# The forgetting attention turns two key tiles in one run and then makes both value products

## The reference, cut to what matters

```python
F = jnp.cumsum(logf, axis=-1)
def block(args):
    qi, Fi, i = args
    logits = (jnp.einsum('bhqd,bhkd->bhqk', qi, k) * scale + Fi[..., :, None] - F[..., None, :])
    logits = jnp.where(kpos[None, :] <= qpos[:, None], logits, -jnp.inf)
    p = jax.nn.softmax(logits, axis=-1)
    return jnp.einsum('bhqk,bhkd->bhqd', p, v)
...
y_f = h_f.reshape(B, S, F_W) * jax.nn.silu(f_z)
y = jnp.concatenate([y_m, y_f], axis=-1) @ w_out[l]
```

## Time and profile before

| | |
|---|---|
| Time, median of 3 runs | 1593.19 us (1592.62 to 1593.48) |
| Span of the profiled execution (no other time is on record for it) | 1588.2 us |
| TensorE, matmul | 1515.7 us busy, 95% |
| TensorE, weight load | 1152.1 us, 73% |
| VectorE | 792.8 us, 50% |
| ScalarE | 533.7 us, 34% |
| POOL | 174.9 us, 11% |
| Mean granted TensorE clock | 0.985 |
| Share of the chain that ended last: scores, turns, products of the attention | 7%, 7%, 8% |

### The profile page before, as it was taken

How to read it: one execution, slowest core, us unless ns; L and a number is a source line. 1 busy time by engine, 2 the same in 40 slices (tenths; PEclk the granted TensorE clock), 3 DMA queues, 4 the chain that set the end, 5 groups by cost and what they waited for, 6 DMA issues and landing times.

```text
span 1588.2 us, 21410 instructions
## 1 busy us (share of the span) xinstructions
PE 1515.7 (95%) x7913; PEld 1152.1 (73%) x7913; DVE 792.8 (50%) x1835; ACT 533.7 (34%) x812; POOL 174.9 (11%) x237
## 2 busy tenths in 40 slices
PE   2999999999899999999999899999999997999998
PEld 2677877887788888888888665555555555888886
DVE  5845445321120100355541585766766747677674
ACT  4842323201111111222211566565655644222220
POOL 2000000002000000000000312103112000222121
PEclk8999999999999999999999999999999998999999
DMA  9313133241341311121232534223161037576761
GB/s 346 133 32 131 68 132 112 101 145 34 107 149 61 99 67 65 42 79 53 79 132 80 151 102 133 54 75 126 45 177 46 16 91 241 175 189 184 182 198 54
DMA packets 128569, 178.09 MB, mean 112 GB/s; under 512 B 8764, under 2 KB 90824, under 8 KB 123416
## 3 DMA queue, kind: packets, MB, share of 16 engines
q1 hardware_dynamic: 119488, 129.75, 27.5%
q0 software_dynamic: 9008, 47.36, 7.9%
HBM read 116.93 MB, written 60.16 MB: 112 GB/s over the span
## 4 chain that ended last, share of the span: by engine, by line
PE 80%; DVE 8%; ACT 5%; DMA 3%; issue 2%; POOL 1%; SPq 0%; DVEq 0%; POOLq 0%; ACTq 0%
PE a_ps_u L703 26%; PE a_ps_u L745 14%; PE m_ps_out L1804 11%; PE f_ps_o L1341 8%; PE f_ps_t L1316 7%; PE f_ps_s L1304 7%; PE a_ps_u L727 1%; DVE stage L481 1%; DVE u_copy L547 1%; DVE stage L555 1%; ACT work L928 1%; PE m_ps_m L1779 1%; ACT work L930 1%; PE m_ps_m L1780 1%; PE m_ps_m L1783 1%
## 5 line engine op out<-in xcount | busy, mean ns | idle before, releaser
L703 PE MATMUL a_ps_u<-a_h_hi,w_in_hi 128*128 128x512 f32 x736 | 286.9, 390 | 0.9 <-DVEq L519 0.9
L703 PE MATMUL a_ps_u<-a_h_lo,w_in_hi 128*128 128x512 f32 x736 | 286.6, 389 | 0.0
L703 PE MATMUL a_ps_u<-a_h_hi,w_in_lo 128*128 128x512 f32 x736 | 198.1, 389 | 0.0
L703 PEld LDWEIGHTS a_ps_u<-a_h_hi,w_in_hi 128*128 128x128 f32 x736 | 138.1, 188 | 31.8 <-issue 3.2
L703 PEld LDWEIGHTS a_ps_u<-a_h_hi,w_in_lo 128*128 128x128 f32 x736 | 138.2, 188 | 28.8
L703 PEld LDWEIGHTS a_ps_u<-a_h_lo,w_in_hi 128*128 128x128 f32 x736 | 138.2, 188 | 28.2
L745 PE MATMUL a_ps_u<-v_hi,a_h_hi 128*128 128x512 f32 x384 | 150.5, 392 | 6.4 <-ACT stage L957 6.4
L745 PE MATMUL a_ps_u<-v_hi,a_h_lo 128*128 128x512 f32 x384 | 150.3, 392 | 0.0
L437 DVE CAST w_in_hi<-w_in_land 128x1024 fp32r<-128x1024 f32 x24 | 16.6, 691 | 178.4 <-PE a_ps_u L703 93.5
L1474 ACT ACTIVATE f_probs_t<-f_ps_t 128x512 f32<-128x512 f32 (+1 forms) x128 | 65.2, 548 | 98.4 <-PE f_ps_t L1316 98.4
L957 ACT ACTIVATE stage<-a_ps_u 128x512 f32<-128x512 f32 x48 | 28.3, 597 | 198.8 <-PE a_ps_u L745 196.8
(11 more groups left out here) (291 smaller groups left out, 2695.8 us busy)
## 6 DMA issues: line engine op xcount, KB each, us to landing
scratch_arrays<-stage POOLq DMA_DIRECT2D x27, 1024.0 KB, 4.6
scratch_qkT<-stage POOLq DMA_DIRECT2D x8, 2048.0 KB, 7.7
w_in_land<-in_w_in SPq DMA_DIRECT2D x24, 512.0 KB, 7.2
w_in_land<-scratch_arrays SPq DMA_DIRECT2D x32, 256.0 KB, 4.8
m_x_in<-in_x SPq DMA_DIRECT2D x16, 512.0 KB, 4.6
out<-m_result SPq DMA_DIRECT2D x15, 512.0 KB, 3.0
a_ada_rows<-in_w_ada SPq DMA_DIRECT2D x3, 2048.0 KB, 16.5
w_in_land<-in_w_in SPq DMA_DIRECT2D x24, 256.0 KB, 3.3
```

What stands on the lines that cost most here:

```text
L703: ins = pe.matmul(ps_u[:, par, b, :], w[:, k, :], h[:, k, cols], start=(k == 0 and i < 2 * len(blocks) and h is h_hi), stop=(k == KT - 1 a ...
```

## The change

TensorE goes through the steps in groups of two, 2g and 2g+1. In a group it turns steps 2g+2 and 2g+3 in one run and then makes products 2g and 2g+1. If both steps have scores, those of step 2g come before the turns and those of step 2g+1 between the two products; if step 2g has none, or a block ends with the group, all scores of the group come first. So that two steps can be turned ahead, there is a third buffer `probs_t_2`, and `BUFFER[s]` is s modulo 3 below step 150 and s modulo 2 from there on (where, for TensorE, only one step is turned before the first product). A copy of step s waits for the last product that read its buffer (`LAST_READ`). The room for the third buffer comes from `gate_z`, which has two slots of 512 columns instead of four; the z of a block is loaded two blocks ahead, after the block that had its slot was stored. VectorE and ScalarE follow in groups of two steps as well: on VectorE `output`, the first share's logits and `invert` still come first, then the copies of both steps with `gate` behind those of key tile 2, then the second share's logits. The waits for `finished` move from product 0 to the copies of step 1.

```diff
+def z_slot(pair, J):
+    return (pair * TB + J) % 2
...
-    return fox["first_z"] if (pair, J) == (0, 0) else fox["gate_z"][:, J * NB:(J + 1) * NB]
+    slot = z_slot(pair, J)
+    return fox["first_z"] if (pair, J) == (0, 0) else fox["gate_z"][:, slot * NB:(slot + 1) * NB]
...
+        ALL_BUFFERS_UNTIL = EARLY_FROM + 3
+        BUFFER = [s % (len(probs_t) if s < ALL_BUFFERS_UNTIL else 2) for s in range(len(STEPS))]
+        LAST_READ = [max((i + 1 for i in range(s) if BUFFER[i] == BUFFER[s]), default=0) for s in range(len(STEPS))]
...
+        def block_ends(g):
+            return 2 * g + 2 < len(STEPS) and STEPS[2 * g + 2][2] == 0
+
+        def shares(g):
+            first, second = share(2 * g), share(2 * g + 1)
+            return ([*first, *second], []) if block_ends(g) or not first else (first, second)
+
+        def turned_in(g):
+            return [s for s in (2 * g + 2, 2 * g + 3) if s < len(STEPS)]
...
+            def load_next_z(n, J):
+                after_next = group_index(n, J) + 2
+                if 2 < after_next < PAIRS * GROUPS:
+                    load_fox_z(sp, scratch, fox, *divmod(after_next, GROUPS))
...
# TensorE
-            turn(*STEPS[0])
-            for s, step in enumerate(STEPS):
-                more = s + 1 < len(STEPS)
-                if s == EARLY_FROM:
-                    pe.wait_ge(s_used, HP * len(CHUNKS_OF))
-                memory_early(s)
-                new = share(s)
-                for m in new:
-                    scores(m)
-                if more:
-                    turn(*STEPS[s + 1])
-                product(s, *step)
+            for s in range(2):
+                turn(*STEPS[s])
+            for g in range(len(STEPS) // 2):
+                memory_early(2 * g)
+                before, between = shares(g)
+                for m in before:
+                    scores(m)
+                in_turn = turned_in(g)
+                together = len(in_turn) if 2 * g + 2 < ALL_BUFFERS_UNTIL else 1
+                for s in in_turn[:together]:
+                    turn(*STEPS[s])
+                product(2 * g, *STEPS[2 * g])
+                for s in in_turn[together:]:
+                    turn(*STEPS[s])
+                for m in between:
+                    scores(m)
+                product(2 * g + 1, *STEPS[2 * g + 1])
+                if 2 * g + 1 == EARLY_FROM:
+                    pe.wait_ge(s_used, HP * len(CHUNKS_OF))
+                memory_early(2 * g + 1)
...
# VectorE
-            copies(0)
-            for s, (n, J, kt) in enumerate(STEPS):
-                if kt == 0 and s:
-                    output(*STEPS[s - 1][:2])
-                for m in share(s):
-                    logits(m)
-                if kt == 0:
-                    invert(n, J)
-                if s + 1 < len(STEPS):
-                    copies(s + 1)
-                if kt == INV_AT - 1:
-                    gate(n, J)
-                memory_early(s)
+            for s in range(2):
+                copies(s)
+            for g in range(len(STEPS) // 2):
+                n, J, kt = STEPS[2 * g]
+                if kt == 0 and g:
+                    output(*STEPS[2 * g - 1][:2])
+                before, between = shares(g)
+                for m in before:
+                    logits(m)
+                if kt == 0:
+                    invert(n, J)
+                for s in turned_in(g):
+                    copies(s)
+                    if STEPS[s][2] == INV_AT:
+                        gate(*STEPS[s][:2])
+                for m in between:
+                    logits(m)
+                for s in (2 * g, 2 * g + 1):
+                    memory_early(s)
...
# ScalarE
+            for g in range(len(STEPS) // 2):
+                if block_ends(g):
+                    for row in EXPS[2 * g] + EXPS[2 * g + 1]:
+                        exponential(*row)
+                for i, s in enumerate(turned_in(g)):
+                    copies(s)
+                    if not block_ends(g):
+                        for row in EXPS[2 * g + i]:
+                            exponential(*row)
+                for s in (2 * g, 2 * g + 1):
+                    memory_early(s)
```

More of the change, by code:

```diff
@@ L1063, in forgetting_heads @@
         stage_1 = keep["stage"][:, 1]
-        probs_t = [sb("probs_t", [P, HP, NB])[:, :, :], heads(keep["work"][:, HP * NB:2 * HP * NB])]
+        probs_t = [sb("probs_t", [P, HP, NB])[:, :, :], heads(keep["work"][:, HP * NB:2 * HP * NB]), fox["probs_t_2"][:, :, :]]
         inv_wide = stage_1[:, 3 * NB:4 * NB].rearrange("p (r h d) -> p r h d", r=QT, h=HP)
@@ L1212, in _ @@
             load_fox_v(sp, scratch, fox, 1, 0)
-            for J in range(2, GROUPS):
-                load_fox_z(sp, scratch, fox, 0, J)
+            load_fox_z(sp, scratch, fox, 0, 2)
             def store_y(n, J):
@@ L1341, in product @@
                     ins = pe.matmul(ps_o[h * F_DH:(h + 1) * F_DH, first:], v_tok[:, kt, h, :],
-                                    probs_t[s % 2][:, h, first:], start=(kt == 0), stop=(kt == key_tiles(J) - 1))
+                                    probs_t[BUFFER[s]][:, h, first:], start=(kt == 0), stop=(kt == key_tiles(J) - 1))
                 ins.then_inc(pv_done, 1)
@@ L1399, in copies @@
                         dve.wait_ge(t_psum, u + 1)
-                        if s >= 2:
-                            dve.wait_ge(pv_done, s - 1)
-                        dve.tensor_copy(probs_t[s % 2][:, h, first:], ps_t[:, u % T_BANKS, first:]
+                        if s == 1:
+                            dve.wait_ge(after["finished"], U_TILES + 4)
+                        if LAST_READ[s]:
+                            dve.wait_ge(pv_done, LAST_READ[s])
+                        dve.tensor_copy(probs_t[BUFFER[s]][:, h, first:], ps_t[:, u % T_BANKS, first:]
                                         ).then_inc(taken_by_dve, 1)
@@ L1471, in copies @@
                         act.wait_ge(t_psum, u + 1)
-                        if s >= 2:
-                            act.wait_ge(pv_done, s - 1)
-                        act.activation(probs_t[s % 2][:, h, first:], ps_t[:, u % T_BANKS, first:], ACT.Copy
+                        if s == 1:
+                            act.wait_ge(after["finished"], U_TILES + 4)
+                        if LAST_READ[s]:
+                            act.wait_ge(pv_done, LAST_READ[s])
+                        act.activation(probs_t[BUFFER[s]][:, h, first:], ps_t[:, u % T_BANKS, first:], ACT.Copy
                                        ).then_inc(copied_by_act, 1)
@@ L1485, in _ @@
             act.preload_act_table_set("natural_log_exp_and_others")
-            copies(0)
-            for s in range(len(STEPS)):
-                due = s + 1 < len(STEPS) and STEPS[s + 1][2] == 0
-                if due:
-                    for row in EXPS[s]:
-                        exponential(*row)
-                if s + 1 < len(STEPS):
-                    copies(s + 1)
-                if not due:
-                    for row in EXPS[s]:
-                        exponential(*row)
-                memory_early(s)
+            for s in range(2):
+                copies(s)
+            for g in range(len(STEPS) // 2):
+                if block_ends(g):
+                    for row in EXPS[2 * g] + EXPS[2 * g + 1]:
+                        exponential(*row)
+                for i, s in enumerate(turned_in(g)):
+                    copies(s)
+                    if not block_ends(g):
[3 more added lines that the diff above has]
+                    memory_early(s)
             act.wait_ge(y_ready, PAIRS * GROUPS)
```

19 lines of the change are left out of this document (7 added, 12 removed).

## The result

The changed kernel takes 1633.82 us (median of five runs, 1630.40 to 1635.96) against 1593.48 for the kernel before (five runs): a ratio of 1.0245 [1.0231, 1.0259], slower by 40 us. The prediction said 1607.5 us, 1592 to 1621: the sign was right, the size was not, and the measured time lies 13 us above the range. The profiled execution has a span of 1628.7 us, 40.5 over the span of before, so the two traces can be compared directly.

A forecast was written before the change was run, and what follows sets the result against it. TensorE, 98% busy from 915 to 1289 us, was taken as the bound. Terms -19.8 + 23.3 + 4.2 + 2 + 1 + 3.7 = +14.4 us on the 1593.2 us median; forecast 1607.5 us, range 1592 to 1621.

The forecast's parts named there:

- saved ends: Attention loop's groups of two steps: fewer ends of transpose and product runs, 0.30 us in most groups, gain 19.8 us.
- inverses' wait: At block starts TensorE's turn of the inverses waits for VectorE's chain from `output` to the wide copy, 23.3 us added.
- ScalarE's copies: TensorE waits for PSUM banks freed by ScalarE: 4.2 us behind exponentials at three pairs' block ends, 2 us in other runs.
- opening: Pair 0: turn 4 moves ahead of product 2, which used to precede a wait for exponentials; 1 us (0 to 3).
- tail: From step 147, memory heads' parts run two steps at a time; gate's sum, moments and chunk 1 come later, 3.7 us.
- buffers, loads, moved waits: Later z loads, smaller `gate_z` and `finished` waits moved to step 1's copies were put at no cost.
- the first rival: At block starts the wait isn't there and the saved ends win: 1584 us, chance 0.12.
- a second product behind the first pays its ends again: Rival on paired products: the joint saves nothing, gain only 11.1 us, time 1616 us; chance 0.13.
- I take 0.03 for 60 runs: Other transpose runs: three banks make the fourth head wait slightly for ScalarE's copy, 2 us in all (0 to 6).
- stays about as it is: Near the third block's end: the wait for exponentials of width 2048, most of 3.0 us, was to remain unchanged.
- the clock rival: At block starts the clock falls after idle among transposes, 3 us in each of 14 blocks: 1650 us, chance 0.07.
- the prediction's own last sign: In the attention: the prediction is wrong if the granted clock drops between 915 and 1289 us.

## Why the prediction had the sign and missed the size

| term | predicted | measured |
|---|---|---|
| saved ends | -19.8 (0.30 in most groups; 17.7 in the middle) | 0.26 in the group shown, 0.25 inside blocks, 0.20 on the average of the middle's 66 groups; 13.1 in the middle |
| inverses' wait | 23.3 | 26.0 in the waits |
| ScalarE's copies (4.2 + 2) | 6.2 | 10.0 (13.6 less 3.6) |
| score slots | 0 | 2.4 |
| clock | 0 | 2.8 to 3.4 in the middle |
| opening | 1 | 7.8 like for like in the profile (5.2 of inverses' waits in it), 5 to 8 by its experiment |
| tail | 3.7 | 10.6 like for like in the profile, 10.7 by the tail in single steps |
| buffers, loads, moved waits | 0 | -1 (a ratio of 0.9995, within its interval) |

The measured terms overlap in places (the inverses' waits of the opening stand in two rows), so they aren't to be added up.

**Right: what decides.** The wait for the inverses outweighs the saved ends; 23.3 us was sized from VectorE's chain and TensorE's cover, and 26.0 came, 2.1 of it in block 0, which the sum left out. Moving `invert` took it away. Against the first rival ("the block-start wait isn't there") stand 1.5 to 2.2 us in 15 of the 16 blocks (0.6 in the last) where under 0.65 would have been needed.

**Right: the joint.** Two products in a row take 1.87 us; the rival "a second product behind the first pays its ends again" would have 2.0. Its bound came from a row at half clock with 256 columns and held at full clock with 512: the joint costs 0.91 where the two passes are 0.85. The rule of the Trainium skill (TensorE: Matmul & The Clock Gate, Part 3), that a weight load overlaps a running matmul only if it goes to other rows, which stands there beside an exception for a background weight buffer, is not what this trace shows: transposes that use all rows, with a weight load of 0.14 us each, come every 0.109 us. The time lies where the kind of operation changes.

**Wrong in size: the saved ends.** "I take 0.30 a group" is near what the group shown above saves (0.26), but over the middle's 66 groups 13.1 us came instead of 17.7. The joint of two products isn't free (0.06 us); what else is missing in the groups at block starts and ends wasn't taken apart.

**Wrong: the tail.** The step that failed is "3.7 us (1 to 6)". It counted VectorE's queue only (the gate's sum, the moments, chunk 1). The wait for ScalarE's copy behind `m_rstd`, 3.0 us, is not in it, and the gate's sum was 2.6 instead of 1.3. In place of 3.7 us there are 10.7.

**Wrong: the opening.** "Turn 4 now stands before product 2 ... 1 us" priced one moved turn. But turns 2 and 3 also stand before product 0, which starts 5.3 us later in the profile (897.7 to 903.0), and what follows doesn't make it up. The inverses' wait of block 0, 2.1 us, is here too. In place of 1 us there are 5 to 8.

**Wrong: small waits in the middle.** "I take 0.03 for 60 runs" was the guess between 0 and 6. With three banks and a fourth use in every run, a copy that is late by a few tenths holds TensorE: delays of 0.45 us at step 46, 0.25 at 48, 0.65 at 50, 0.25 at 76 (pair 1; the other pairs are much the same), none of which I had looked up, though ScalarE's queue could have been written out for each group as I did for step 42. There the sum said 1.4 and 1.05 came. One step was plainly misread: the wait behind the exponentials of width 2048 near the end of the third block "stays about as it is". It was 0.76 us a pair and became 1.35, with 0.27 more behind it: 3.4 us in four pairs, a third of the 10.0. The score slots' wait (0.40 us at step 42) was put at nothing because the slots weren't touched; but two turns in a row delay VectorE's copies, and those stand before the logits that free the slots.

**Half right: the clock rival.** It said 3 us in each of 14 blocks, and it had a chance of 0.07. By the prediction's own last sign, "if the granted clock drops between 915 and 1289", it was wrong here. The granted clock fell in the middle at 1094.4 and 1261.6 us, 0.1 and 1.2 us behind the end of inverses' waits of 1.72 and 2.19 us, for 3.4 us each; TensorE there, kernel after:

```profile
1260.47 0.66 PE L1347 MATMUL f_ps_t<-ident,stage 128*128 128x128 f32 x4 [2.19 <-DVE stage L1443]
...
1262.16 1.97 PE L1364 MATMUL f_ps_o<-work,v_tok 128*64 128x512 f32 x4
1263.93 1.58 PE L1364 MATMUL f_ps_o<-probs_t,v_tok 128*64 128x512 f32 x4
```

Two products take 3.28 us here to the next scores (1265.44), at granted clock 0.50, that is the 1.2 GHz level, and 1.87 at full clock; a 3.4 us stretch at half pace is worth 1.7, so a fall costs 1.4 to 1.7 us. Before the second fall TensorE had done eight transposes, waited, and done ten; before the first it had done eight, waited, and just begun on the inverses. The kernels with the tail or the opening in single steps show two and four such falls, each from 0.3 us before the end of a wait of 1.8 to 2.2 us to 0.9 behind it. In the ten kernels without the inverses' wait, the one before among them, the granted clock is 1.00 in every stretch from 925 to 1278 us. That is a strong correlation; what separates the two or four blocks with a fall from the others, whose waits were as long, I did not settle.

Together: the middle's delays are 35.2 us more than before, 26.4 were predicted, and its gain is 13.1 instead of 17.7. That is the 13.3 us missing there, but for the rounding. Like for like, the opening misses about 5.3 and the tail 7.4.

**What stays open.** The opening's cost isn't known better than 5 to 8 us, since its experiment had clock falls of its own. The tail's waits were undone together, not one by one, and its granted clock (0.83 from 1320 to 1370 us; before, 0.85 from 1320 to 1365) isn't separated from them. And no kernel here has a fourth bank, so that the small waits come from the three banks is argued from the queues and not tried.

## What to carry to other kernels

Grouping steps of a pipelined loop saves the ends of runs, here a quarter of a microsecond a group, and takes a step of cover away from every wait that a group contains. So write out, for each group that begins or ends something (a block's output, its normalization, a moved copy), each engine's queue from the releasing instruction to the awaited one, and group only where no such chain crosses: 40 groups of the right kind made the kernel 9 us faster, all 80 made it 40 us slower. When a producer's chain is what is late, look at what stands in its queue ahead of the awaited result without being needed for it. And the waits of 0.2 to 1.4 us for ScalarE's copies and for score slots, most of which had not been looked up, together took 12.4 us of their own, about as much as the 13.1 gained in the middle. Last, when two orders of work are compared from one instruction to another, count what each has done by then: here twenty transposes, 2.2 us, had moved across the line.

## What was not expected of the hardware

A product right behind a product of the same shape costs 0.06 us beyond its columns (0.91 against 0.85), while the two ends of a run of scores, transposes or products, where the kind of operation changes, cost 0.15 to 0.2 together. And idle stretches of 1.7 to 2.2 us among transposes were in some cases followed by 3.4 us at half clock (granted clock 0.50), though the 3.73 us of idle in the earlier trace rows was followed by 6.7.
